# Input projection on raw x in a decoder-block kernel: scaled weights, 1/rms and shift at the results, adaLN rows spread over three phases

## The reference

```
mod = silu(c) @ w_ada + b_ada                    # 6 x 1024: shift_m, scale_m, gate_m, shift_f, scale_f, gate_f
h = rms_norm(x, norm_mix) * (1 + scale_m) + shift_m
proj = h @ w_in                                  # 928 columns: 512 for S5, 256 c_q, 128 c_kv, 32 k_rope
y_ssm = s5_group(u_ssm, ...)                     # complex diagonal state space model, then GELU and a gated unit
y_attn = mla_group(c_q, c_kv, k_rope_raw, ...)   # q, k, v from c_q and c_kv, then causal attention
x = x + gate_m * (concat(norm(y_ssm), norm(y_attn)) @ w_out)
h2 = rms_norm(x, norm_ffn) * (1 + scale_f) + shift_f
out = x + gate_f * peer_ffn(h2, ...)             # 8 heads x 16 experts fetched for each position
```

## Time and profile before

| | us |
|---|---|
| median of 3 runs | 3123.32 (3122.87 to 3129.01) |
| profiled execution, its own time | 3138.7 |
| its span, first to last instruction | 3136.9 |
| `phase_ab` within it | 0 to 180.4 |
| `phase_c` | 180.4 to 298.2 |
| `phase_d` | 298.2 to 365 |
| `phase_ef` | 365 to the end |

### The profile page before, as it was taken

How to read it: one execution, slowest core, us unless ns; L and a number is a source line. 1 busy time by engine, 2 the same in 40 slices (tenths; PEclk the granted TensorE clock), 3 DMA queues, 4 the chain that set the end, 5 groups by cost and what they waited for, 6 DMA issues and landing times.

```text
span 3136.9 us, 38313 instructions
## 1 busy us (share of the span) xinstructions
PE 2323.5 (74%) x13074; PEld 1913.2 (61%) x13074; DVE 2216.8 (71%) x5297; ACT 2031.5 (65%) x3762; POOL 1295.7 (41%) x1165
## 2 busy tenths in 40 slices
PE   3989868888786986767666777677677667777666
PEld 2665547777675555666555666666566556666555
DVE  8972658888884776777776676667676766677654
ACT  3214437888785675776667666766676666766765
POOL 1000323444443454444444445444444444444443
PEclk8979989998887986776778676777776776677766
DMA  6501159999999999999999999999999999999997
GB/s 258 196 31 49 74 218 400 420 393 375 366 397 417 409 409 420 421 421 421 421 421 416 421 420 418 414 422 417 416 417 415 421 418 418 410 421 420 418 421 324
DMA packets 174613, 1159.41 MB, mean 370 GB/s; under 512 B 22641, under 2 KB 23553, under 8 KB 42961
## 3 DMA queue, kind: packets, MB, share of 16 engines
q0 software_dynamic: 148352, 1077.61, 83.3%
q1 hardware_dynamic: 25376, 77.25, 6.6%
q10 hardware_dynamic: 688, 2.10, 0.2%
HBM read 1146.27 MB, written 9.44 MB: 368 GB/s over the span
## 4 chain that ended last, share of the span: by engine, by line
DMA 32%; DVE 24%; PE 17%; ACT 10%; issue 4%; POOL 1%; POOLq 0%; DVEq 0%; ACTq 0%
DMA pair<-in_experts_dram,idx_g 31%; DVE pair L1846 11%; PE acc_a L1474 5%; ACT pair L1623 4%; PE pef L1449 3%; PE acc_b L1474 2%; ACT L1619 1%; ACT w L1621 1%; PE pef L1367 1%; POOL pair L1305 1%; DVE top_i L1774 1%; PE acc_b L1348 1%; DVE staged L1775 1%; DVE top_i L1777 1%; PE acc_b L1397 1%
## 5 line engine op out<-in xcount | busy, mean ns | idle before, releaser
L1305 POOL DMA_INDIRECT pair<-in_experts_dram,idx_g x1024 | 1231.6, 1203 | 1418.1 <-PE acc_a L1474 771.8
L1846 DVE SCALAR_TENSOR_TENSOR pair<-pair,h 128x1024 f32<-128x1024 f32 x1024 | 1246.1, 1221 | 636.5 <-DMA pair<-in_experts_dram,idx_g 619.2
L1623 ACT ACTIVATE pair<-pair,w 128x1024 f32<-128x1024 f32 x1024 | 1176.4, 1149 | 33.3
L1474 PE MATMUL acc_a<-ident,pair 128*128 128x128 f32 x5120 | 857.9, 329 | 381.8 <-ACT pair L1623 370.6
L1474 PEld LDWEIGHTS acc_a<-ident,pair 128*128 128x128 f32 x5120 | 726.7, 171 | 504.6 <-ACT pair L1623 470.5
L1474 PE MATMUL acc_b<-ident,pair 128*128 128x128 f32 x3072 | 587.7, 359 | 293.3 <-ACT pair L1623 288.9
L1474 PEld LDWEIGHTS acc_b<-ident,pair 128*128 128x128 f32 x3072 | 483.8, 186 | 390.1 <-ACT pair L1623 380.1
L1619 ACT ACTIVATE ga<-a 128x1 f32<-128x1 f32 x1024 | 204.2, 199 | 670.4 <-DVE pair L1846 650.5
L1621 ACT ACTIVATE w<-ga,g 128x1 f32<-128x1 f32 x1024 | 301.7, 295 | 33.2
L1449 PE MATMUL pef<-h2t,wq 128*128 128x128 f32 x1536 | 200.5, 294 | 0.0
L1449 PEld LDWEIGHTS pef<-h2t,wq 128*128 128x128 f32 x1536 | 199.6, 213 | 1.0 <-issue 1.0
(11 more groups left out here) (361 smaller groups left out, 2319.0 us busy)
## 6 DMA issues: line engine op xcount, KB each, us to landing
wada<-in_w_ada_t_dram SPq DMA_DIRECT2D x48, 512.0 KB, 5.5
pair<-in_experts_dram,idx_g POOLq DMA_INDIRECT x1024
pieces<-in_w_query_t_dram SPq DMA_DIRECT2D x18, 512.0 KB
wq<-in_w_query_t_dram SPq DMA_DIRECT2D x4, 2048.0 KB, 29.1
out_dram<-h SPq DMA_DIRECT2D x8, 512.0 KB
wout_b<-in_w_out_dram SPq DMA_DIRECT2D x1, 4096.0 KB, 34.2
ht<-in_x_t_dram ACTq DMA_DIRECT2D x2, 1024.0 KB, 11.5
ht<-in_x_t_dram SPq DMA_DIRECT2D x2, 1024.0 KB, 10.4
```

What stands on the lines that cost most here:

```text
L1305: p.indirect_dma_start(pair[n % R], None, A["experts"], bass.IndirectOffsetOnAxis(ap=idx[:, t % (2 * PH), k:k + 1], axis=0)).then_inc(pair ...
L1474: last = t.matmul(accs[ACC[i]][:, k * P:(k + 1) * P], pair[n % R][:, D + k * P:D + (k + 1) * P], S.ident[:], is_transpose=True, start=n % ...
L1623: s_.activation(pair[n % R][:, D:], pair[n % R][:, D:], ACT.Copy, scale=w[:, n % NA:n % NA + 1]).then_inc(scaled, 1)
L1846: v.scalar_tensor_tensor(down, down, 1.0, h2[:, n // P, :], ALU.mult, ALU.mult, accum_out=a[:, n % NA:n % NA + 1]).then_inc(dotted, 1)
```

## The change

- **Projection on raw x.** x is no longer touched. The rows of `win_m` are scaled by `a_m` = (1 + scale_m) * norm_mix into `wm_scaled` (ACT, one `k` at a time), those of `win_s` in place. 1/rms comes in when the results leave PSUM, as a scalar for each position, together with shift_m @ w_in, which `shift_sum` makes on DVE in 16 steps and `shift_rows` sums over partitions on PE: `z_evict` for the 416 columns, `u_evict` for the 512, both on DVE. For `u_evict` 1/rms goes through DRAM (`r_kept`, `r_step`) into another order.
- **Order.** Each `k` of the first four position tiles starts as soon as its `wm_scaled` is there. The additions of `sqx` go to POOL. All loads of x and `win_m` stand in SP's queue among the rows. The latents are scaled in place in `z_lat` and transposed from there. `toep` lies now where `pr` and `pi` were (`place` at 16 and 24), so it is zeroed after the eighth `turn_p`.
- **Tables.** `rr`, `ri`, `pr`, `pi` are made four steps at once.
- **Modulation rows.** `phase_ab` keeps the 16 rows of shift_m and scale_m. 24 go to `phase_c` and 8 to `phase_d`.

```diff
+            for n, (first, end) in enumerate(PIECES):
+                row_load(first)
+                sp.dma_start(ht[:, first:end, :], xt[:, first:end, :]).then_inc(x_and_wm_in[n], 16)
+                sp.dma_start(win_m[:, first:end, :], w_of[:, first:end, DS:]).then_inc(x_and_wm_in[n], 16)
+                for k in range(first + 1, end):
+                    row_load(k)
+            for n in range(KD, 2 * KD):
+                row_load(n)
...
+            sp.wait_ge(r_ready, 1)
+            sp.dma_start(r_kept.rearrange("(i p) -> p i", p=P), rx[:, 1, :], allow_slow_non_contiguous=True).then_inc(r_moved, 16)
+            sp.wait_ge(r_moved, 16)
+            sp.dma_start(r_step[:], r_kept.rearrange("(c j) -> c j", j=L)).then_inc(r_moved, 16)
...
-            pool.wait_ge(w_used, 4)
-            pool.dma_start(win_m[:], w[:, :, DS:]).then_inc(wm_in, 16)
-            pool.wait_ge(w_used, EARLY)
-            pool.dma_start(win_s[:], w[:, :, 0:DS]).then_inc(ws_in, 16)
-            nc.gpsimd.memset(S.toep[:], 0.0).then_inc(toep_zero, 1)
+            for k in range(1, KD):
+                pool.wait_ge(sq_ready, k + 1)
+                if k >= 2:
+                    pool.wait_ge(sq_added, k - 1)
+                nc.gpsimd.tensor_tensor(sqx[:, 0], sqx[:, 0], sqx[:, k], ALU.add).then_inc(sq_added, 1)
+            pool.wait_ge(w_used, KD + 2)
+            pool.dma_start(win_s[:], w_of[:, :, 0:DS]).then_inc(ws_in, 16)
...
+            pool.wait_ge(p_t, 8)
+            nc.gpsimd.memset(S.toep[:], 0.0).then_inc(toep_zero, 1)
...
+                s.activation(sqx[:, k], ht[:, k], ACT.Square).then_inc(sq_ready, 1)
+                act.wait_ge(am_ready, k + 1)
+                s.activation(wm_s[:, k, :], win_m[:, k, :], ACT.Copy, scale=S.a_m[:, k:k + 1]).then_inc(wms_ready, 1)
...
-                    last = s.activation(hk, hk, ACT.Identity, scale=S.a_m[:, k:k + 1], bias=S.mod[:, SHIFT_M + k:SHIFT_M + k + 1])
...
-            pe.wait_ge(ident_made, 1)
-            pe.wait_ge(rstd_ready, 1)
-            for i in range(NT):
-                last = t.matmul(rb[:, tile(i)], rx[:, 1, i:i + 1].to_broadcast([P, P]), S.ident[:], start=True, stop=True)
-            last.then_inc(row_done, 1)
...
+                pe.wait_ge(wms_ready, k + 1)
+                for i in range(WIDE):
+                    last = t.matmul(mla_bank[i][:, 0:MW], ht[:, k, tile(i)], wm_s[:, k, :], start=k == 0, stop=k == KD - 1)
+                    if k == KD - 1:
+                        last.then_inc(mla_done, 1)
+            mla(4)
+            mla(5)
+            square_sums()
+            shift_rows(0)
+            mla(6)
+            shift_rows(1)
+            pe.wait_ge(z_ready, 1)
+            mla(7)
+            project_u(0)
+            project_u(1)
...
+                weigh_row(k)
+                dve.wait_ge(w_used, k + 1)
+                b = SCALE_M + k
+                ch.step(v.tensor_tensor(S.mod[:, b:b + 1], S.mod[:, b:b + 1], S.vec[:, V_BA + b:V_BA + b + 1], ALU.add))
+                v.scalar_tensor_tensor(S.a_m[:, k:k + 1], S.mod[:, b:b + 1], 1.0, S.vec[:, V_NM + k:V_NM + k + 1], ALU.add, ALU.mult).then_inc(am_ready, 1)
+            for n in range(KD, 2 * KD):
+                weigh_row(n)
...
+            def shift_sum(weights, at_, to):
+                for k in range(KD):
+                    o, sh = acc_w[:, at_:to], S.mod[:, SHIFT_M + k:SHIFT_M + k + 1]
+                    if k == 0:
+                        ch.step(v.tensor_scalar(o, weights[:, k, :], sh, None, ALU.mult))
+                    elif k < KD - 1:
+                        ch.step(v.scalar_tensor_tensor(o, weights[:, k, :], sh, o, ALU.mult, ALU.add))
+                    else:
+                        v.scalar_tensor_tensor(o, weights[:, k, :], sh, o, ALU.mult, ALU.add).then_inc(shift_acc, 1)
+
+            shift_sum(win_m, DS, DPROJ)
+            dve.wait_ge(ws_in, 16)
+            shift_sum(win_s, 0, DS)
...
-            dve.wait_ge(row_done, 1)
-            for k in range(KD):
-                v.tensor_tensor(ht[:, k], ht[:, k], rb[:], ALU.mult).then_inc(xn_ready, 1)
-                weigh_row(KD + k)
...
-                for k in range((3, 5)[n], KD):
-                    hk = ht[:, k, halves(n)]
-                    last = v.tensor_scalar(hk, hk, S.a_m[:, k:k + 1], S.mod[:, SHIFT_M + k:SHIFT_M + k + 1], ALU.mult, ALU.add)
-                last.then_inc(hd_ready, 1)
...
+            def z_evict(i):
+                dve.wait_ge(mla_done, i + 1)
+                v.scalar_tensor_tensor(z_of[:, i], mla_bank[i][:, 0:MW], rx[:, 1, i:i + 1], swb[:, DS:], ALU.mult, ALU.add).then_inc(z_ready, 1)
...
+                v.scalar_tensor_tensor(up[:, :, L - 1 - j, :], u_bank[j % 4][:].rearrange("p (g c) -> p g c", c=C), r_step[:, j:j + 1],
+                                       swb[:, 0:DS].rearrange("p (g c) -> p g c", c=C), ALU.mult, ALU.add).then_inc(u_out, 1)
...
+            for k, n in ((0, 4), (4, 4), (8, 1)):
+                ch.mark(v.tensor_tensor(t4[0], on_steps(ct[:, 0], n), powers(0, k, n), ALU.mult))
+                ch.mark(v.tensor_tensor(S.rr[:, :, k:k + n, :], t4[0], t4[1], ALU.subtract))
...
-            for b in range(EARLY, 32):
-                weigh_row(b)
...
+            sp.dma_start(wfour[:], w[:, FIRST_ROW:FIRST_ROW + 4, :]).then_inc(row_in[0], 16)
+            sp.wait_ge(x_ready, 8)
+            for n in range(1, ROWS // 2 - 1):
+                if n >= 3:
+                    sp.wait_ge(row_used, 2 * n - 2)
+                sp.dma_start(wrow[(n - 1) % 3][:], w[:, FIRST_ROW + 2 * n + 2:FIRST_ROW + 2 * n + 4, :]).then_inc(row_in[n % 3], 16)
...
+            weigh_rows(0, 4)
             groups_out(1)
             groups_out(3)
             steps_out(1)
+            weigh_rows(4, 6)
             groups_out(5)
             steps_out(3)
+            weigh_rows(6, 8)
             groups_out(7)
             steps_out(5)
             steps_out(7)
...
             for b in range(8):
+                weigh_rows(8 + 2 * b, 10 + 2 * b)
...
+                    n, b = i // 2, GATE_F + i
+                    dve.wait_ge(row_in[n % 2], 16 * (EARLIER // 6 + n // 2 + 1))
+                    wb = wrow[n % 2][:, i % 2]
+                    v.scalar_tensor_tensor(wb, wb, 1.0, S.silu_c[:], ALU.mult, ALU.mult, accum_out=S.mod[:, b:b + 1]).then_inc(row_used, 1)
```

More of the change, by code:

```diff
@@ L159, in phase_ab @@
     ones = place(nc, "ones_b", [P, P], 86.5)
-    macc = small("macc", [P, 48], FP32)
-    junk = place(nc, "junk_b", [P, QL + KL], 87)
+    junk = place(nc, "junk_b", [P, 2, QL + KL], 87)
     rx = small("rx", [P, 2, NT], FP32)
+    r_step = small("r_step", [P, L], FP32)
+    r_kept = nc.dram_tensor("r_kept", (SEQ,), FP32, kind="Internal").ap()
+    PIECES = ((0, 1), (1, 3), (3, 5), (5, 8))
+    PIECE_OF = [n for n, (first, end) in enumerate(PIECES) for _ in range(first, end)]
     st = small("stat_b", [P, NT, 4], FP32)
@@ L296, in _ @@
-            ct_evict(NT - 1)
             def k_evict(n):
@@ L376, in turn_p @@
                 else:
-                    pe.wait_ge(k_ready, 2)
                     pe.wait_ge(k_out, m + 2)
@@ L382, in turn_p @@
                 last.then_inc(p_t, 1)
-            pe.wait_ge(ws_in, 16)
-            for j in range(L):
-                if j >= 2:
-                    pe.wait_ge(u_out, j - 1)
-                for k in range(KD):
-                    last = t.matmul((u0, u1)[j % 2], ht[:, k, j::L], win_s[:, k, :], start=k == 0, stop=k == KD - 1)
-                last.then_inc(u_done, 1)
-                if j == 0:
-                    kernels(3)
-                if j in (1, 3):
-                    for m in range(4):
-                        turn_p(2 * (j - 1) + m)
+            for k in range(KD):
+                pe.wait_ge(wms_ready, k + 1)
+                for i in range(WIDE):
+                    last = t.matmul(mla_bank[i][:, 0:MW], ht[:, k, tile(i)], wm_s[:, k, :], start=k == 0, stop=k == KD - 1)
+                    if k == KD - 1:
+                        last.then_inc(mla_done, 1)
+            mla(4)
[8 more added lines that the diff above has]
+            project_u(1)
+            for i in (0, 1, 2):
+                turn_latents(i)
+            project_u(2)
+            for i in (3, 4, 5):
+                turn_latents(i)
+            project_u(3)
+            for i in (6, 7):
+                turn_latents(i)
+            pe.wait_ge(k_ready, 1)
+            pe.wait_ge(z_ready, NT)
+            kernels(0)
+            pe.wait_ge(ct_out, NT)
+            for n in (1, 2):
+                kernels(n)
+            project_u(4)
+            kernels(3)
+            project_u(5)
+            pe.wait_ge(k_ready, 2)
+            for m in range(8):
+                turn_p(m)
+            project_u(6)
+            project_u(7)
             pe.wait_ge(u_out, L)
@@ new lines, in u_evict @@
+            def u_evict(j):
+                if j == 0:
+                    dve.wait_ge(shift_out, 2)
+                    dve.wait_ge(r_moved, 32)
```

(15 more changed lines are left out.)

354 lines of the change are left out of this document (185 added, 169 removed).

## The result

Over 20 executions the changed kernel took 3108.2 us (median; 3103.7 to 3126.5), the kernel before 3126.7 (3113.4 to 3142.8) in the 20 beside them. The ratio is 0.9946, with a 95% interval of 0.9931 to 0.9960: 17 us faster, between 12.5 and 21.6. I had forecast 32 us less, and the median lies 11 us above the forecast's own range, 3085 to 3097. The profiled execution of the changed kernel took 3121.9 us, 16.8 less than that of before.

The account below looks back on a forecast made before the run. phase_ab was taken as PE waiting until 56.4 us, then working nearly throughout. Terms -34.7 (phase_ab), +2.4 (phase_c) and +0.3 (phase_d) gave -32.0, so 3091.3 us from a median of 3123.3; own range 3085 to 3097, wider range 3076 to 3110.

Parts of the forecast that it names:

- What bounds the kernel: phase_ab: a wait, then a long run of PE; shortening it needs PE to start before 56.4 or do less behind.
- I let it cost nothing: phase_ab: POOL's seven sqx additions could hold DVE up 6 to 19 us, but were counted as 0.
- the 3.5 of the rival: phase_ab: POOL holds DVE up by one addition and a late row, 3.5 us, total 3095; chance 0.05.
- The rule: phase_ab: by the skill page, each POOL addition reading SBUF would stop a DVE row with two SBUF inputs.
- The eighth tile at 60.5: phase_ab: PE's banks come free at 60.5 us, with seven of eight mla tiles, 39 us of work, done by then.
- The other terms of phase_ab: phase_ab: shift_sum 12.1 us, PE behind the eighth tile's start 62.1, toep's zeroing to phase end 23.1; tables nothing, 1/rms hidden.
- The loads: phase_ab: 16.9 MB needed for the shift at 392 GB/s, 43.1 us, all there by 46.1 us.
- forecast +2.4: phase_c: the two rows ahead of groups_out(7) make PE wait 2.4 us more; ends 0 and 7.3.
- forecast +0.3: phase_d: one row per tile costs 0 within 1.0 us of slack; the bias add at the end costs 0.3 us.
- Should the slack be POOL's or ACT's: phase_d: if the slack belongs to POOL or ACT, the rows cost eight times 0.5, +4 us.
- The 15.4 us: Whole kernel: profiled execution 3138.7 against median 3123.3, a difference of 15.4 us applied to the median.
- phase_c at another clock: phase_c: full clock in timed runs of both kernels 3096, only the changed one 3070, only the one before 3117; chance 0.24 together.

Follow-up runs that it names:

- e1: Changed kernel with POOL's seven additions of sqx left out (wrong numbers): phase_ab 146.3 us against 152.7, ratio to the kernel before 0.9926.
- e3: Changed kernel with PE's shift product for the 416 columns moved behind the seventh position tile: phase_ab 149.8 us, ratio to the kernel before 0.9937.
- e9: Changed kernel with sqx additions on DVE, shift product behind the seventh tile, and phase_c rows behind copies PE awaits: phase_ab 150.1 us, ratio to before 0.9893.
- e8: Changed kernel without the 32 rows of phase_c and phase_d and their loads: phase_c 117.8 us, phase_d 67.1 us, ratio to the kernel before 0.9942.

## Why the prediction was wrong

**What bounds the kernel** held. The wait of 27.3 us went, and PE's start at "about 10 us" was 11.3.

**The step that failed** is "I let it cost nothing", of POOL's seven additions, with its ground "until 46 us DVE is paced by the loads: 16 rows and the small work are 25 us of 46". Busy time was set against elapsed time, as if the loads ran on whatever DVE did. They don't: from the sixth row on SP's queue waits for a row buffer ahead of each load of a row. A late row is a late load, as the times of issue in e1 and in the changed kernel show. The cost was 6.4 us (152.7 against 146.3 in e1), not 0, and not the 3.5 of the rival, to which I gave 0.05. The additions took 2.35 to 3.41 us each, the middle case above the forecast's upper bound ("three times that", 2.7). The 14 us by which they held DVE up lie within its 6 to 19, which it named and then dropped.

The rule spoke right. The Trainium skill, "SBUF — State Buffer", "Who interferes with whom", says that a DVE instruction with two SBUF inputs contends with a GpSimd instruction that reads SBUF; its section "Summary: rules for kernel authors" adds that the second one to issue is blocked until the first ends. The trace agrees: a 128x1 addition took 2.17 us instead of 0.16 beside POOL's, and POOL's product in `phase_d` 1527 ns instead of 615 beside a row.

**The eighth tile at 60.5** had a second omission: "By 60.5 PE has done seven of the eight `mla` tiles" counted work without the queue. The product of the shift stands on PE ahead of the seventh tile and waits for the last row. e3 gives its price, 2.9 us, part of it the same microseconds as those of POOL's. With both edits, in e9, the phase is no shorter than in e3. (The working has a tile as half of 16 records; it is all 16, and the 5.6 us that it uses is right: 67.57 to 73.16.)

**The other terms of phase_ab** were right: `shift_sum` took 11.1 us from first to last (12.1), PE behind the eighth tile 62.7 (62.1), the chain of `toep` to the end 22.4 (23.1). The tables and 1/rms through DRAM cost nothing; PE never waited for `k_ready` or `r_step`. The loads were right only in their effect, as said under e1.

**phase_c**, forecast +2.4: the wait came in the size worked out (2.23 us), though at the turned block and beside the 1.36 us that stayed. I had left out the clock behind it, 2.3 us, and 0.8 us at the very end of the phase, half of it PE's last products at the low level. With the long low clock +5.6, with the short +3.5, with none +7.2. The forecast's ends, 0 and 7.3, held all three.

**phase_d**, forecast +0.3: e8 shows 2.5, of which 1.6 are PE's clock at the two ends, which the forecast had not in its sum. The other 0.9 is POOL's product beside a row, once, at the last tile. The forecast named this case ("Should the slack be POOL's or ACT's") and set it aside.

**The 15.4 us** between the profiled execution and the median I had taken for a constant to subtract. It is chance: three profiled executions of the kernel before took between 3129.9 and 3138.7 us, which differ by the length of the low clock and by `phase_ef`. The rival "phase_c at another clock" was real and was no matter of one kernel against the other: both have executions of both kinds, and of the changed kernel's 20 times 13 lie below 3109 and 6 above 3120.

The sum with what the runs showed: -34.7 + 6.4 (POOL) + 0.5 (the rest of the first phase) = -27.8; + 5.6, + 2.8 and + 2.5 gives -16.9, against 16.8 less in the profiled execution. The 2.5 of `phase_ef` in this pair is within its scatter. That the ratio gives 17 as well is in part luck, since most executions are of the kind with the short stretch, for which the terms of the first three phases give about 22.

## What to carry to other kernels

Before work with two inputs goes to POOL, look at what DVE does at that time; it is not free there even when DVE has idle time, if DVE's instructions give buffers back to a queue of loads. Follow each engine's queue by its waits and not by its sum of work: one product that waits for the last input, written ahead of a tile that could run, cost 3 us here. And where times of one program fall in two groups, take several profiles before an offset or a phase is used in a sum.
